# Rotary embeddings of a two-layer hybrid decoder: halves turned by SBUF transfers in place of permutation products

## The chip, the cores and the metric

One core of a Trainium2 chip runs the whole program. The metric is the device time of one execution in microseconds. The kernel before took 964.73 us (median of 3 runs, 963.35 to 967.94). The instructions run on five engines: PE (TensorE, its weight loads shown apart as PEld), DVE (VectorE), ACT (ScalarE), POOL (GpSimd) and SP (SyncE), which here only starts transfers.

## The reference

Two layers over 256 positions of width 1024, in float32. Each layer has a mixer sub-layer with three branches (a linear recurrence, retention, latent attention) that share one input projection, then a gated MLP. Three tensors of the mixer are rotated by position:

```python
def apply_rope(x, cos, sin):
    half = x.shape[-1] // 2
    x1, x2 = x[..., :half], x[..., half:]
    return jnp.concatenate([x1 * cos - x2 * sin, x1 * sin + x2 * cos], axis=-1)

q = apply_rope(q.reshape(b, s, 8, 64), cos, sin)      # retention, halves of 32
k = apply_rope(k.reshape(b, s, 8, 64), cos, sin)
k_rope = apply_rope(kr, cos, sin)                     # latent attention, one key of 32, halves of 16
q_rope = apply_rope(q_rope, cos, sin)                 # eight queries of 32, halves of 16
```

## The kernel before

Activations lie with features on the 128 partitions and the 256 positions along the row. Every dense product is made of three products of float32r parts (a high and a low part of the weights, the same of the activations), so each 1 MB block of weights is loaded into one of three `raw` slots by SP, split into `w_hi` by ACT (line 598) and `w_lo` by DVE (line 1097), and then used by PE (line 1697). A slot is loaded again when the low part of its block is made (`lo_ready`), and its high part is overwritten when PE has used it (`blk_used`). SP's list of loads (line 480) is in the order of the blocks, and each of its waits holds everything behind it. The order of work on every engine is written out by hand. The blocks of a mixer layer are, by number: 0, 1 values; 2, 3 retention queries; 4, 5 retention keys; 6, 7 recurrence inputs (`lx`); 8, 9, 10 latents (`c`), the last one with the rotary key; 11, 12 retention gates (`g`); 13, 14 recurrence gates (`lg`); 15, 16 latent queries up (`uq`); 17 latent keys and values up (`ukv`); 18 on: merge gates and output projections by turns. A block of 256 columns is `two_tiles`, 48 products.

The rotation. For the retention queries and keys there are four pairs of tiles, 0 to 3, which PE leaves in banks 2, 4, 5 and 0. DVE multiplies a pair by the cosines into `AB` and by the sines into one of two halves of `tmp` (`rope_parts`, lines 1305 and 1306). PE multiplies `tmp` with a signed permutation table (`rotate`, line 1809, a float32 product of 512 columns) into the bank it came from, and DVE adds that bank to `AB` (`rope_sum`, line 1311). `rotate(0)` and `rotate(1)` stand ahead of block 6 on PE, `rotate(2)` ahead of block 7, `rotate(3)` ahead of block 8. DVE's order around them is: split 5, parts 1, split 6, split 7, parts 2, sum 0, parts 3, sum 1, (in layer 0 the angles of the second table), split 8, taps 0, sum 2, split 9, sum 3, taps 1, split 10. After the splits of blocks 7 to 20 DVE also makes one sum of the modulation (line 1090).

The rotary key follows block 10 (`rotary_key_parts`, lines 1392 and 1393, ahead of split 13; the product on line 1862 behind block 11; `rotary_key_sum`, line 1398, behind the first two score tiles). The rotary queries follow block 16 (`rotary_q_parts`, lines 1457 and 1458, ahead of split 19; the product on line 1962; `rotary_q_sum`, line 1463, between `variance(0)` and `variance(1)`, both line 1469). ACT spreads each variance over a tile (line 854), and PE transposes it into a bank (`head_scales`, line 1953) with the value products between them; `head_scales(1)` is the last thing PE does before the merge gates.

The tables (identity, `center`, `mean64`, the two permutations, the decays and the mask) come in two transfers; the second, 1472 KB, is issued by ACT in layer 0 after split 3.

Of the kernel before, what the change touches and what calls it, by code (L numbers as in the profile page):

```python
# [21 lines left out]
P = 128  # L22
# [4 lines left out]
ALU = mybir.AluOpType  # L27
# [27 lines left out]
def constants(seq):  # L55
# [4 lines left out]
    center = ident - same_head / 64.0  # L60
    mean64 = same_head / 64.0
    ones = np.ones((P, P))

    def rotation(dim):
        half = dim // 2
        r = np.zeros((P, P))
        for m in range(P):
            if m % dim < half:
                r[m + half, m] = -1.0
            else:  # L70
                r[m - half, m] = 1.0
        return r
# [8 lines left out]
    inv_ret = (ROPE_THETA ** (-np.arange(0, 64, 2) / 64.0))[f % 32][:, None]  # L81
    inv_mla = (ROPE_THETA ** (-np.arange(0, 32, 2) / 32.0))[f % 16][:, None]
# [3 lines left out]
    parts = [ident, ones, inv_ret, inv_mla, eps, q_eps, tiny, center, mean64, rotation(64), rotation(32), *decay, mask]  # L86
# [33 lines left out]
def trunk_kernel(nc, A, consts, out):  # L120
# [90 lines left out]
    with ctx:  # L211
# [49 lines left out]
        kr = sb("kr", [P, T])  # L261
        rot_tmp = pbuf[:].rearrange("p a b -> p (a b)")[:, 0:2 * T].rearrange("p (a b) -> p a b", a=2)
# [20 lines left out]
        center, mean64, rot_r, rot_m = (piece(NFIRST + P * i) for i in range(4))  # L283
        c0 = NFIRST + 4 * P
# [44 lines left out]
        rot_ps, rot_t, rot_c, rope = sig("rot_ps", 4), sig("rot_t", 4), sig("rot_c", 4), sig("rope", 4)  # L329
# [17 lines left out]
        kt_ps, kt_t, kt_c, kt = (sig(n, 1) for n in ("kt_ps", "kt_t", "kt_c", "kt"))  # L347
        qt_ps, qt_t, qt_c, qt = (sig(n, 1) for n in ("qt_ps", "qt_t", "qt_c", "qt"))
# [106 lines left out]
        def _(sp):  # L455
# [4 lines left out]
            for n in range(ADA0):  # L460
# [98 lines left out]
        def _(act):  # L559
# [178 lines left out]
            for l in range(L):  # L738
# [39 lines left out]
                act.wait_ge(rot_ps.s, rot_ps.at(l, 4))  # L778
# [238 lines left out]
        def _(dve):  # L1017
# [277 lines left out]
            for l in range(L):  # L1295
# [12 lines left out]
                def rope_sum(i):  # L1308
                    dve.wait_ge(rot_ps.s, rot_ps.at(l, i + 1))
# [379 lines left out]
        def _(pe):  # L1689
# [84 lines left out]
            for l in range(L):  # L1774
# [28 lines left out]
                def rotate(i):  # L1803
                    if i == 0:
                        pe.wait_ge(tables_in, 16)
                        pe.wait_ge(v_ev.s, v_ev.at(l, 4))
# [414 lines left out]
```

## Time and profile before

| | |
|---|---|
| median, lowest, highest of 3 runs | 964.73, 963.35, 967.94 us |
| span of the profiled execution, first to last instruction | 962.9 us |
| PE busy | 944.9 us (98%) |
| DVE busy | 723.5 us (75%) |
| ACT busy | 521.0 us (54%) |
| PE weight loads busy | 881.8 us (92%) |
| transfers | 206.37 MB, 214 GB/s |

The profiled execution is told by its span; what lies around the span is not in the page, and the span is 1.8 us below the median of the runs. Busy time is of one engine, so the shares do not add up. Lines are those of the kernel, and many matmuls have the line of a helper (1697). A row of the timeline has start and duration in us, the engine, the line, the operation, what is written and read, how many instructions are merged in it and, in brackets, how long the engine was idle before it and what ended that. SPq and ACTq are the instructions with which SP and ACT start transfers. The two layers run through the mixer 463.9 us apart.

### The profile page before, as it was taken

Reading aid. Unit: us, or ns where it says so; the run is one execution under the profiler, and the core shown is the slowest. Engines: PE = TensorE matmul, PEld = TensorE weight load, DVE = VectorE, ACT = ScalarE, POOL = GpSimd, SP = SyncE. Lnnn points to the kernel's source line nnn. Section 1 sums busy time; section 2 is a strip of 40 time slices with the busy share of each in tenths; the row PEclk is TensorE's granted clock in tenths of the full one; section 3 lists DMA queues with packets and bytes.
Section 4 is the critical chain, followed back from the end, with each engine's and each line's share of the span. In section 5 each row is a group of like instructions: output and inputs, shape, how many; then the busy total and the mean of one; then the engine's idle time right before and its main releaser. Section 6 shows DMA issues by size and latency. Waiting matters only on the chain.

```text
span 962.9 us, 17659 instructions
## 1 busy us (share of the span) xinstructions
PE 944.9 (98%) x6956; PEld 881.8 (92%) x6956; DVE 723.5 (75%) x966; ACT 521.0 (54%) x693; POOL 43.5 (5%) x85
## 2 busy tenths in 40 slices
PE   7999999999999999999999999999999999999997
PEld 7889999999998999999979999999999799999996
DVE  4869968867687878887786976887668787676666
ACT  4345856436457655454673475743445675554553
POOL 0000000100000000000000000000000000000000
PEclk7799999999999999999999999999999999999999
DMA  9986668765584676766546775767657555655451
GB/s 354 328 258 213 229 214 259 244 222 198 179 291 121 233 248 249 252 242 202 203 160 180 244 245 182 245 207 256 201 180 251 175 175 175 208 181 178 144 201 47
DMA packets 134427, 206.37 MB, mean 214 GB/s; under 512 B 6496, under 2 KB 104800, under 8 KB 134240
## 3 DMA queue, kind: packets, MB, share of 16 engines
q1 hardware_dynamic: 122704, 162.08, 51.2%
q0 software_dynamic: 11520, 41.95, 11.9%
q10 hardware_dynamic: 144, 1.51, 0.5%
q8 instruction: 43, 0.70, 0.3%
q14 instruction: 16, 0.13, 0.0%
HBM read 204.47 MB, written 1.05 MB: 213 GB/s over the span
## 4 chain that ended last, share of the span: by engine, by line
PE 89%; DVE 4%; DMA 3%; ACT 1%; issue 1%; SPq 1%; DVEq 0%; ACTq 0%
PE banks L1697 79%; DMA h<-in_ada_rows 1%; DVE w_lo L1097 1%; DMA raw<-in_w_in 1%; PE banks L1713 1%; PE banks L1979 1%; PE banks L1982 1%; PE banks L1721 1%; SPq L463 1%; PE banks L1827 1%; PE banks L1809 1%; PE banks L1989 1%; PE banks L1727 1%; PE banks L1846 1%; DVE EF L1599 1%
## 5 line engine op out<-in xcount | busy, mean ns | idle before, releaser
L1697 PE MATMUL banks<-h_lo,w_hi 128*128 128x256 f32 x1504 | 425.9, 283 | 2.0 <-DVE w_lo L1097 1.8
L1697 PE MATMUL banks<-h_hi,w_lo 128*128 128x256 f32 x1504 | 420.7, 280 | 0.0
L1697 PE MATMUL banks<-h_hi,w_hi 128*128 128x256 f32 x1504 | 420.6, 280 | 0.0
L1697 PEld LDWEIGHTS banks<-h_lo,w_hi 128*128 128x128 f32 x1504 | 283.5, 188 | 5.4 <-DVE w_lo L1097 2.2
L1697 PEld LDWEIGHTS banks<-h_hi,w_lo 128*128 128x128 f32 x1504 | 283.5, 188 | 2.3 <-issue 1.4
L1697 PEld LDWEIGHTS banks<-h_hi,w_hi 128*128 128x128 f32 x1504 | 283.4, 188 | 0.0
L1097 DVE TENSOR_TENSOR w_lo<-raw,w_hi 128x2048 fp32r<-128x2048 f32 x96 | 219.3, 2289 | 51.2 <-ACT w_hi L598 50.9
L598 ACT ACTIVATE w_hi<-raw 128x2048 fp32r<-128x2048 f32 x96 | 182.5, 1912 | 109.8 <-PE banks L1697 85.6
L1599 DVE SCALAR_TENSOR_TENSOR EF<-banks,par,EF 128x254 f32<-128x254 f32 (+1 forms) x176 | 76.8, 478 | 57.2 <-ACT EF L949 52.4
L1623 DVE TENSOR_TENSOR w_lo<-raw,w_hi 128x2048 fp32r<-128x2048 f32 x42 | 96.0, 2285 | 21.5 <-ACT w_hi L968 21.5
L968 ACT ACTIVATE w_hi<-raw 128x2048 fp32r<-128x2048 f32 x42 | 80.4, 1913 | 36.7 <-PE banks L1697 36.7
L949 ACT ACTIVATE EF<-banks,par 128x256 f32<-128x256 f32 x88 | 44.8, 560 | 92.3 <-PE banks L1697 92.3
L1090 DVE SCALAR_TENSOR_TENSOR adw<-adw,cbc 128x1024 f32<-128x1024 f32 x66 | 79.6, 1220 | 1.2 <-DVE h L1537 1.1
L1697 PE MATMUL banks<-w_hi,oa_lo 128*128 128x512 f32 x192 | 75.9, 395 | 0.0
L1697 PE MATMUL banks<-w_hi,oa_hi 128*128 128x512 f32 x192 | 75.9, 395 | 0.0
L1697 PE MATMUL banks<-w_lo,oa_hi 128*128 128x512 f32 x192 | 75.9, 395 | 0.0
L542 POOL DMA_DIRECT2D adw<-in_ada_rows x80 | 42.3, 529 | 694.5 <-DVE adw L1090 493.4
L876 ACT ACTIVATE lat<-banks 128x512 f32<-128x512 f32 x24 | 14.2, 592 | 74.8 <-PE banks L1697 74.8
L1697 PEld LDWEIGHTS banks<-w_hi,oa_hi 128*128 128x128 f32 x192 | 36.1, 188 | 8.6
L1697 PEld LDWEIGHTS banks<-w_lo,oa_hi 128*128 128x128 f32 x192 | 36.1, 188 | 7.9
L1697 PEld LDWEIGHTS banks<-w_hi,oa_lo 128*128 128x128 f32 x192 | 36.1, 188 | 7.8
L1697 PE MATMUL banks<-oa_lo,w_hi 128*128 128x256 f32 x128 | 36.9, 288 | 0.0
(277 smaller groups left out, 1242.5 us busy)
## 6 DMA issues: line engine op xcount, KB each, us to landing
raw<-in_w_in SPq DMA_DIRECT2D x52, 1024.0 KB, 5.5
raw<-in_ffn_w_up SPq DMA_DIRECT2D x44, 1024.0 KB, 5.1
adw<-in_ada_rows POOLq DMA_DIRECT2D x80, 512.0 KB, 4.8
raw<-in_ffn_w_down SPq DMA_DIRECT2D x22, 1024.0 KB, 4.8
raw<-in_w_out SPq DMA_DIRECT2D x8, 1024.0 KB, 7.3
raw<-in_ret_wo SPq DMA_DIRECT2D x4, 1024.0 KB, 6.2
raw<-in_lru_wo SPq DMA_DIRECT2D x4, 1024.0 KB, 6.8
raw<-in_mla_wo SPq DMA_DIRECT2D x4, 1024.0 KB, 7.5
```

Source lines behind the costliest of these rows:

```text
L463: sp.dma_start(ada0_buf(n), src).then_inc(ada0_landed(n)[0], 16)
L542: pool.dma_start(adw[:, slot, :], ada_v[:, bass.ds(n + ADA0, 1), :].rearrange("p a d -> p (a d)")).then_inc(adw_in[slot], 16)
L598: A_(dst, src, ACT.Copy).then_inc(hi_ready.s, 1)
L876: A_(flat2(lat, m % 2), PS[:, gate_bank(m), :], ACT.Tanh, scale=0.5).then_inc(mg_th.s, 1)
L949: a = A_(EF[:, 2 * part + b, :], PS[:, 4 + part, T * b:T * b + T], ACT.Identity, scale=par[:, l, bass.ds(i * 2 + col["tap2"] + NFF * (1 - ...
L968: A_(w_hi[:, slot, :], raw[:, slot, :], ACT.Copy).then_inc(hi_ready.s, 1)
L1090: V.scalar_tensor_tensor(adw[:, n % 2, :], adw[:, n % 2, :], 1.0, cbc[:], ALU.mult, ALU.mult, accum_out=mraw[:, n % NT:n % NT + 1]).then_i ...
L1097: V.tensor_tensor(dst, whole, hi, ALU.subtract).then_inc(lo_ready.s, 1)
L1599: v = V.scalar_tensor_tensor(EF[:, 2 * part + b, d:T], PS[:, 4 + part, T * b:T * b + T - d], par[:, l, bass.ds(i * 2 + col[f"tap{tap}"] + ...
L1623: V.tensor_tensor(w_lo[:, slot, :], raw[:, slot, :], w_hi[:, slot, :].bitcast(F32), ALU.subtract).then_inc(lo_ready.s, 1)
L1697: ins = MM(ps, lhs, rhs, start=first and n == 0, stop=last and n == 2)
L1713: ins = MM(PS[:, bank, P * i:P * i + P], x[:, c, P * kk:P * kk + P], diag[:, c, :], start=True, stop=True)
```

## The change

The products with permutation tables go. DVE's product with the sines (whose table now has a minus for one half of each head, from negative frequencies) is moved between partitions by SP: for each group of `half` partitions one transfer from SBUF to SBUF takes the other half of the head. That is 4 transfers of 32 partitions for each of the four pairs (`turn`), 8 of 16 partitions for the rotary key and 8 for the rotary queries. DVE then adds the landed tile instead of a bank. `turn(0)` stands in SP's list behind the load of block 7, `turn(1)` behind 8, `turn(2)` and `turn(3)` behind 10, the key's behind 15, the queries' behind 21, each with a wait for DVE's product. PE no longer waits for the sums before it writes a bank again, only for DVE's two reads of it. Three tables of 128 columns leave the constants (`center`, which nothing read, and the permutations).

```diff
-    parts = [ident, ones, inv_ret, inv_mla, eps, q_eps, tiny, center, mean64, rotation(64), rotation(32), *decay, mask]
+    parts = [ident, ones, inv_ret, inv_mla, eps, q_eps, tiny, mean64, *decay, mask]
...
+            def halves_turned(dst, src, half, landed_sig):
+                for p in range(0, P, half):
+                    q = p ^ half
+                    sp.dma_start(dst[p:p + half], src[q:q + half]).then_inc(landed_sig.s, 16)
+
+            def turn(l, i):
+                two = slice(2 * (i % 2), 2 * (i % 2) + 2)
+                sp.wait_ge(rot_t.s, rot_t.at(l, i + 1))
+                if i >= 2:
+                    sp.wait_ge(rope.s, rope.at(l, i - 1))
+                halves_turned(lat[:, two, :], tmp[:, two, :], 32, turn_in[i % 2])
...
+                    for i in {7: (0,), 8: (1,), 10: (2, 3)}.get(j, ()):
+                        turn(l, i)
+                    if j == 15:
+                        sp.wait_ge(kt_t.s, kt_t.at(l, 1))
+                        halves_turned(lat[:, 1, :], lat[:, 0, :], 16, kt_in)
+                    if j == 21:
+                        sp.wait_ge(qt_t.s, qt_t.at(l, 1))
+                        halves_turned(turned_q, rot_tmp, 16, qt_in)
...
-                act.wait_ge(rot_ps.s, rot_ps.at(l, 4))
+                act.wait_ge(rope.s, rope.at(l, 4))
...
                     if i >= 2:
-                        dve.wait_ge(rot_ps.s, rot_ps.at(l, i - 1))
+                        dve.wait_ge(turn_in[i % 2].s, turn_in[i % 2].at(l, 64))
...
-                    dve.wait_ge(rot_ps.s, rot_ps.at(l, i + 1))
+                    dve.wait_ge(turn_in[i % 2].s, turn_in[i % 2].at(l, 64 * (i // 2) + 64))
                     dve.wait_ge(rot_c.s, rot_c.at(l, i + 1))
-                    V.tensor_tensor(AB[:, 2 * i:2 * i + 2, :], AB[:, 2 * i:2 * i + 2, :], rope_bank(i), ALU.add).then_inc(rope.s, 1)
+                    V.tensor_tensor(AB[:, 2 * i:2 * i + 2, :], AB[:, 2 * i:2 * i + 2, :], lat[:, 2 * (i % 2):2 * (i % 2) + 2, :],
+                                    ALU.add).then_inc(rope.s, 1)
...
-                    dve.wait_ge(kt_ps.s, kt_ps.at(l, 1))
+                    dve.wait_ge(kt_in.s, kt_in.at(l, 128))
...
-                    dve.wait_ge(qt_ps.s, qt_ps.at(l, 1))
+                    dve.wait_ge(qt_in.s, qt_in.at(l, 128))
...
-                    MM(PS[:, (2, 4, 5, 0)[i], :], rot_r, flat2(tmp, i % 2), start=True, stop=True).then_inc(rot_ps.s, 1)
-                rotate(0)
-                rotate(1)
+                pe.wait_ge(v_ev.s, v_ev.at(l, 4))
                 two_tiles(l, J[("lx", 0)], 3)
-                rotate(2)
                 two_tiles(l, J[("lx", 1)], 1)
-                rotate(3)
-                pe.wait_ge(rope.s, rope.at(l, 2))
+                heads_taken(1)
                 two_tiles(l, J[("c", 0)], 4)
...
-                MM(PS[:, 2, 0:T], rot_m, lat[:, 0, :], start=True, stop=True).then_inc(kt_ps.s, 1)
...
-                MM(PS[:, 4, :], rot_m, rot_tmp.rearrange("p a b -> p (a b)"), start=True, stop=True).then_inc(qt_ps.s, 1)
```

`heads_taken(i)` waits for the two products of pair `i` on DVE. The turned queries land in `ptb`, the turned pairs in `lat` rows 0 to 3, the turned key in `lat` row 1.

## Rows read from the trace of the kernel before

**Rows 1.** The page, part 1: busy us, share of the span, instructions.

```profile
PE 944.9 (98%) x6956; PEld 881.8 (92%) x6956; DVE 723.5 (75%) x966; ACT 521.0 (54%) x693; POOL 43.5 (5%) x85
```

**Rows 2.** Windows: stretch, length; busy per engine; granted clock, DMA share, GB/s.

```profile
0.00:44.00 44.00, 36.59 (x157) 33.13 (x158) 29.28 (x58) 20.21 (x34) 1.57 (x6) 0.73 0.92 337
...
72.00:96.00 24.00, 24.00 (x193) 22.71 (x192) 23.38 (x50) 13.34 (x18) 1.58 (x3) 1.00 0.65 217
```

**Rows 3.** Chain of work, layer 1: start us, us on the chain, what.

```profile
534.86 1.72 PE banks L1809 x4
...
542.18 0.86 PE banks L1809 x2
...
549.55 11.21 PE banks L1697 x96
...
575.42 0.43 PE banks L1862 x2
...
613.22 0.86 PE banks L1962 x2
...
618.22 0.44 PE banks L1953 x4
```

**Rows 4.** The same chain in layer 0.

```profile
70.97 1.72 PE banks L1809 x4
...
85.61 11.21 PE banks L1697 x96
...
98.54 5.61 PE banks L1697 x48
```

**Rows 5.** Timeline of DVE, layer 0.

```profile
63.45 0.68 DVE L1306 TENSOR_TENSOR tmp<-banks,sinr 128x512 f32<-128x512 f32 x1
...
72.92 0.68 DVE L1305 TENSOR_TENSOR AB<-banks,cosr 128x512 f32<-128x512 f32 x1
...
80.94 2.28 DVE L1097 TENSOR_TENSOR w_lo<-raw,w_hi 128x2048 fp32r<-128x2048 f32 x1
...
95.89 1.22 DVE L1106 TENSOR_TENSOR w_lo<-raw,w_hi 128x1024 fp32r<-128x1024 f32 x1
...
106.86 0.42 DVE L1393 TENSOR_TENSOR lat<-banks,sinm 128x256 f32<-128x256 f32 x1
...
113.86 0.41 DVE L1398 TENSOR_TENSOR kr<-kr,banks 128x256 f32<-128x256 f32 x1
```

**Rows 6.** Timeline of DVE, layer 1, the split of block 9.

```profile
547.41 2.28 DVE L1097 TENSOR_TENSOR w_lo<-raw,w_hi 128x2048 fp32r<-128x2048 f32 x1
```

**Rows 7.** Timeline of DVE, layer 1, around the rotary queries.

```profile
611.22 0.68 DVE L1458 TENSOR_TENSOR pbuf<-banks,sinm 128x512 f32<-128x512 f32 x1
...
615.29 0.63 DVE L1463 TENSOR_TENSOR AB<-AB,banks 128x512 f32<-128x512 f32 x1
615.84 0.19 DVE L1469 RECIPROCAL var_rc<-var_sd 128x8 f32<-128x8 f32 x1
```

**Rows 8.** Timeline of ACT in the same stretch.

```profile
615.41 1.30 ACT L854 ACTIVATE lat<-var_rc 128x512 f32<-128x512 f32 x2 [0.23 <-DVE var_rc L1469]
```

**Rows 9.** Timeline of SP: transfers started one behind the other.

```profile
1.33 0.42 SPq L457 DMA_DIRECT2D cst<-shape_constants  x1
1.79 0.43 SPq L459 DMA_DIRECT2D x<-in_x  x1
...
512.00 1.28 SPq L491 DMA_DIRECT2D wbd<-in_lru_wx  x2
```

**Rows 10.** Transfers: KB each, median us from issue to landing.

```profile
out<-x SPq DMA_DIRECT2D x4, 256.0 KB, 2.0
...
wbd<-in_lru_wx SPq DMA_DIRECT2D x4, 64.0 KB, 5.6
```

**Rows 11.** Timeline of ACT, layer 0, the split of block 4.

```profile
53.56 1.92 ACT L598 ACTIVATE w_hi<-raw 128x2048 fp32r<-128x2048 f32 x1 [10.64 <-DMA raw<-in_w_in]
```

**Rows 12.** Timeline of PE, layer 0, block 4.

```profile
57.86 0.38 PE L1697 MATMUL banks<-h_lo,w_hi 128*128 128x256 f32 x1 [1.76 <-DVE w_lo L1097]
```

More of the change, by code:

```diff
@@ L59, in constants @@
     same_head = (f[:, None] // 64 == f[None, :] // 64).astype(np.float64)
-    center = ident - same_head / 64.0
     mean64 = same_head / 64.0
     ones = np.ones((P, P))
[L64 to L72, printed above, removed]
     t = np.arange(seq)[None, :]
@@ L80, in constants @@
     mask = np.concatenate([diag, np.zeros((P, P)), diag], axis=1)
-    inv_ret = (ROPE_THETA ** (-np.arange(0, 64, 2) / 64.0))[f % 32][:, None]
-    inv_mla = (ROPE_THETA ** (-np.arange(0, 32, 2) / 32.0))[f % 16][:, None]
+    inv_ret = ((ROPE_THETA ** (-np.arange(0, 64, 2) / 64.0))[f % 32] * np.where(f % 64 < 32, 1.0, -1.0))[:, None]
+    inv_mla = ((ROPE_THETA ** (-np.arange(0, 32, 2) / 32.0))[f % 16] * np.where(f % 32 < 16, 1.0, -1.0))[:, None]
     eps = np.full((P, 1), EPS)
@@ L282, in trunk_kernel @@
         inv_ret, inv_mla, eps, q_eps, tiny = (piece(2 * P + i, 1) for i in range(5))
-        center, mean64, rot_r, rot_m = (piece(NFIRST + P * i) for i in range(4))
-        c0 = NFIRST + 4 * P
+        mean64 = piece(NFIRST)
+        c0 = NFIRST + P
         decay = cst[:, c0:c0 + HEADS * T].rearrange("p (h t) -> p h t", h=HEADS)
@@ L328, in trunk_kernel @@
         g_th, g_ev = sig("g_th", 2), sig("g_ev", 2)
-        rot_ps, rot_t, rot_c, rope = sig("rot_ps", 4), sig("rot_t", 4), sig("rot_c", 4), sig("rope", 4)
+        rot_t, rot_c, rope = sig("rot_t", 4), sig("rot_c", 4), sig("rope", 4)
+        turn_in = [sig(f"turn_in{i}", 128) for i in range(2)]
         rs_ps, rs_p, rs_av = sig("rs_ps", 8), sig("rs_p", 8), sig("rs_av", 8)
@@ L346, in trunk_kernel @@
         uv_ps, uv_ev = sig("uv_ps", 1), sig("uv_ev", 2)
-        kt_ps, kt_t, kt_c, kt = (sig(n, 1) for n in ("kt_ps", "kt_t", "kt_c", "kt"))
-        qt_ps, qt_t, qt_c, qt = (sig(n, 1) for n in ("qt_ps", "qt_t", "qt_c", "qt"))
+        kt_in, kt_t, kt_c, kt = sig("kt_in", 128), *(sig(n, 1) for n in ("kt_t", "kt_c", "kt"))
+        qt_in, qt_t, qt_c, qt = sig("qt_in", 128), *(sig(n, 1) for n in ("qt_t", "qt_c", "qt"))
         s_ps, s_m, s_max, s_neg = (sig(n, 4) for n in ("s_ps", "s_m", "s_max", "s_neg"))
@@ L1874, in _ @@
                 ins.then_inc(cs_ps.s, 1)
-                pe.wait_ge(kt.s, kt.at(l, 1))
+                pe.wait_ge(kt_t.s, kt_t.at(l, 1))
+                pe.wait_ge(kt_c.s, kt_c.at(l, 1))
                 two_tiles(l, J[("g", 1)], 2)
@@ L1938, in head_means @@
                 def head_means(i):
+                    if l == 0 and i == 0:
+                        pe.wait_ge(tables_in, 16)
                     pe.wait_ge(rv_sq.s, rv_sq.at(l, i + 1))
@@ L2028, in merge_gate @@
                         ready(l, gj)
-                        sg, n = ((qt, 1), (r_o, 1), (uv_ev, 2), (mg_th, 2))[m] if m < 4 else (mg_th, m - 1)
+                        sg, n = ((qt_t, 1), (r_o, 1), (uv_ev, 2), (mg_th, 2))[m] if m < 4 else (mg_th, m - 1)
                         pe.wait_ge(sg.s, sg.at(l, n))
+                        if m == 0:
+                            pe.wait_ge(qt_c.s, qt_c.at(l, 1))
                     wh, wl = weights(l, gj)
```

20 lines of the change are left out of this document (9 added, 11 removed).

## The prediction

> **What bounds the kernel now.** I read the page's busy times first: PE is busy for 98% of the span, DVE for 75% [rows 1]. The windows then say whether the stretches with the rotations are like the whole. From 72 to 96 us PE is busy for all of 24.00 us at the full granted clock, but DVE for 23.38 of 24, far over its mean [rows 2]. So in layer 0 the cover for DVE's work is thin just where the change takes PE's work away. The chain of waits gives what a product is worth: it runs through PE in both layers, and a piece's length on it is what PE would gain without the piece [rows 3, 4]. The timelines of DVE, ACT, PE and SP then say who is late next.
>
> **What the change removes.** On the chain two rotations take 1.72 us and a single one 0.86 [rows 3]; there are four per layer, 3.44 us. The key's product takes 0.43, the queries' 0.86 [rows 3]. That is 4.73 us per layer and 9.46 in both, if everything else were early enough. It is not, so I follow the places where PE must meet somebody.
>
> **Layer 1, up to the queries.** Without rotations block 8 could start at 549.55 - 3.44 = 546.11 [rows 3] and block 9 half a pair of blocks (11.21 / 2 = 5.60) later, at 551.7. DVE makes the low part of block 9 by 547.41 + 2.28 = 549.69 [rows 6], and it is DVE's own full list that sets this time, not PE. PE arrives 2 us later than that, so nothing is lost: 3.44 us gained. Behind block 11 the waits of DVE and ACT are for PE's products, so they move with it, and the key's 0.43 comes on top: 3.87 us.
>
> **Layer 0, up to the queries.** Here DVE has the angles of the second table to make between sum 1 and split 8. PE ends the keys at 70.97 [rows 4]. Blocks 6 and 7 run directly, 2 x 5.60, to 82.2. The low part of block 8 is ready at 80.94 + 2.28 = 83.22 [rows 5], so PE starts it at about 83.3 and ends block 9 at 94.5 or a little later. The two gate products before block 10 take 1.73 (98.54 less the end of the pair of blocks, 85.61 + 11.21 = 96.82 [rows 4]), to 96.2, and block 10 is ready at 95.89 + 1.22 = 97.11 [rows 5]. DVE's full list sets that one too. It starts at 97.15 where it started at 98.54 [rows 4]: 1.39 us of the 3.44 are kept, and 2.05 lost to DVE. With the key's 0.43 that is 1.82. All this goes with DVE's list unmoved, which needs the turned halves to be there in time.
>
> **Do the turns land in time?** The trace has no transfer from SBUF to SBUF, so I bound them. An issue on SP: two ordinary ones stand 0.46 us apart (1.33 and 1.79), two of the 64 KB blocks with a more broken pattern take 1.28, 0.64 each [rows 9]. I take 0.5. From issue to landing: 2.0 us for a plain store of 256 KB on a quiet queue, 5.6 for 64 KB right behind a 1 MB load [rows 10]. `turn(1)` is issued once DVE's sine product of pair 1 is done, at 63.45 + 0.68 = 64.13 in layer 0 [rows 5], behind load 8; `turn(0)` is a pair earlier. With 4 x 0.64 and the 5.6 us turn 1 is there at 72.3. Its first reader, parts 3, stands behind parts 2 and sum 0, at 72.92 + 3 x 0.6 = 74.7 [rows 5]. Turns 2 and 3 have two splits and more between product and sum. I take zero; if turn 1 needs the 10.64 us that ACT once waited for a load [rows 11], it lands at 77.3, 2.6 us late, and that is the other end. The load behind the turns: 256 KB more on the queue is 0.26 / 0.337 = 0.8 us at the rate of the first window [rows 2]. That is block 8's in both layers; SP issues it more than two splits of DVE's list ahead of its own, so I take zero, with 0.8 as the end. The key's eight: issued from 106.86 + 0.42 = 107.28, the last at 107.3 + 3.5 = 110.8, landed at 112.8. Its sum starts at 113.86 before [rows 5] and can now move up by less than 1 us. So zero too, up to 0.5. DVE's sums have two SBUF inputs instead of SBUF and a bank; operations of this size that read a bank take 0.63 to 0.68 [rows 7], and I change nothing for it.
>
> **The rotary queries are the place where it costs.** I work in layer 1's old time, since all engines arrive shifted alike. DVE's product is done at 611.22 + 0.68 = 611.90 [rows 7]. SP has by then issued load 21 and stands at the wait. The eighth transfer is issued at 611.9 + 7 x 0.5 = 615.4 and lands 2.0 later, at T = 617.5 with a little for the semaphore. The sum was due at 615.29 [rows 7]. DVE stands for 2.2 us, and behind it stands `variance(1)`, 0.55 after the sum's start, 0.19 long [rows 7]; ACT then needs 0.65 for its tile (1.30 for two [rows 8]), with about 0.16 for the two handovers. So `head_scales(1)` on PE starts at T + 1.55 = 619.05, where it started at 618.22 [rows 3]. The 0.86 us of the product are gone and 0.83 on top. The bounds: with 0.64 per issue and 5.6 to landing T is 622.0 and the loss 5.3. On the good side a transfer that never touches HBM could be quicker than any row, and the end is the product's whole 0.86 gained; less is likely even then, since ACT's two tiles, ready at 615.41 + 1.30 = 616.7 [rows 8], are themselves set by DVE. What is late next behind it is the low part of block 20, which follows the second `group_norm`: two operations of DVE of 0.7 and a split of 2.28 [rows 5], 3.7 us, while PE has the first merge gate to do, a block of 5.6. Load 22, pushed back by up to 2 us, is for the merge product after the next.
>
> The trace shows that SP's transfers are issued without waiting for one another's landing [rows 9]. The Trainium skill, page "DMA: Bandwidth & Descriptors", section "Rules for kernel authors", says that many small transfers should be coalesced, since "under 64 KB you're paying mostly overhead", and these are of 16 and 32 KB; section "Anatomy of one DMA" puts the fixed part at about 2.0 us. If the eight paid that one after the other, the sum would be the third rival's, by an estimate from that page 16.6 us for the eight; if they overlap as the rows' issues do, it stays as above.
>
> **The constants.** 3 x 64 KB less in the second table, on the same engines as the loads of blocks 4 and 5. ACT waits 10.64 us for block 4 in layer 0 [rows 11], and PE 1.76 behind it [rows 12]. 0.196 MB at 337 GB/s [rows 2] is 0.58 us; I take 0.5, between 0 and 0.6. It moves PE and DVE alike, so it adds to the above.
>
> **The sum.** Layer 0: 0.5 + 1.82 - 0.83 = 1.5. Layer 1: 3.87 - 0.83 = 3.0. Together 4.5 us off the profiled span of 962.9, 958.4; the median of the runs lies 1.8 above the span, so 964.7 - 4.5 = 960.2. Best of the bounds: 6.2 + 2 x 0.86 + 0.1 = 8.0 off, 956.7. Worst: 0 for the constants, 5.7 - 2 x 5.3 - 0.5 - 2.6 - 0.8 = 8.8 slower, 973.5.
>
> **Rivals.**
> 1. PE's whole 9.46 us come back, 955.3. It needs DVE's list in layer 0 to be looser than it looks, and the queries to land before 615.3. For it speaks only the 98% [rows 1]; against it the ends of the splits [rows 5] and the 3.4 us between product and sum [rows 7], less than eight issues. 0.10.
> 2. The queries land late because of the 1 MB load just ahead of them in the same queue, about 4 us after the last issue, midway between the two rows: T about 619.6, loss 2.9 per layer, together 6.2 - 5.8 = 0.4, so 964.3, no change. For it: 5.6 us of the small transfers behind a load [rows 10]. Against it: SP issues load 21 while DVE is still before its two products, so that load should be nearly through when the eighth is issued. 0.20.
> 3. Slower: each of the eight takes the fixed 2.0 us [rows 10] in turn and not side by side. T is 627.9, `head_scales(1)` 629.5, 11.2 us lost per layer: 6.2 - 22.4 = 16.2 slower, 981. It becomes a loss from the point where T passes 619.8 (618.22 + 3.1 - 1.55), that is from 0.81 us per issue on with 2 us for the last landing. This is the page's rule as a mechanism here. Milder forms of it (around 1.3 us each, 972) are in its chance, 0.10.
> 4. DVE stands at parts 3 in layer 0 for turn 1, by the 2.6 us worked out above, all of it on PE: 962.8. For it: DVE's list has no gap there [rows 2]. Against it: 2.4 us between the slower landing and the reader. 0.12.
>
> **How the numbers follow.** The forecast has 0.48, with a range of its own from 958 to 962.5. A difference under 0.5% (4.8 us) is about what a measurement of this kernel can't tell from none: that is 959.9 to 969.6. The forecast lies at the edge of it; I put a bit under three fifths of its 0.48 below 959.9 together with rival 1 and a share of the uncertainty of the baseline: faster 0.41. Slower holds the larger part of rival 3: 0.09. The rest, with rivals 2 and 4, is no change: 0.50. The range from 956.5 to 966.0 leaves out rival 3, most of rival 1 and a little of rival 2.
>
> **What would show it.** Right: no PE time on lines 1809, 1862 and 1962; PE waiting in layer 0 for `w_lo` ahead of blocks 8 to 10, some 2 us in all, and not in layer 1; DVE waiting for a transfer at line 1463's sum in both layers, by 2 us or so, and PE waiting before the second set of line 1953; no wait of DVE at the parts and sums of the four pairs. Wrong: a wait of DVE for transfers ahead of the split of block 8; issues on SP over 0.81 us each; PE not waiting at line 1953 at all (then 958 or less); or PE's saved time given back in the MLP, where I assume that everybody follows PE.

## The result and the profile after

The change makes the kernel slower. The changed kernel takes 974.71 us (median of 4 runs, 973.80 to 975.97), the kernel before 964.77 us in the same comparison; the ratio is 1.0101, with a 95% interval of 1.0083 to 1.0119. The forecast was 960.2 us and its range ended at 966.0. The profiled execution has a span of 972.4 us; before it was 962.9. One of the ten executions of e1 below took 1304.61 us at a mean granted clock of 0.65; it moves e1's median by under 0.1 us.

The page's first part, as in [rows 1], and three of its transfer rows (KB each, median us from issue to landing, as in [rows 10]):

```profile
PE 940.3 (97%) x6932; PEld 880.3 (91%) x6932; DVE 723.3 (74%) x966; ACT 520.9 (54%) x693; POOL 43.5 (4%) x85
...
lat<-tmp SPq DMA_DIRECT2D x32, 64.0 KB, 5.6
...
ptb<-pbuf SPq DMA_DIRECT2D x16, 32.0 KB, 4.0
lat<-lat SPq DMA_DIRECT2D x16, 16.0 KB, 3.4
```

PE is busy for 4.6 us less, though 9.46 us of products are gone. A busy time that falls by half of what was taken away says that some of the rest got slower. The span grew by 9.5 us all the same, so PE stands for 14 us more than before.

To see where, I set PE's timelines side by side and took the start of the same product in both. The table has the times of the profiled executions; a minus means that the changed kernel is ahead.

| what PE starts | layer 0, before, after | shift | layer 1, before, after | shift |
|---|---|---|---|---|
| recurrence gates, ahead of block 10 | 96.65, 93.80 | -2.85 | 560.60, 562.79 | +2.19 |
| first score tile | 111.84, 108.88 | -2.96 | 575.78, 577.54 | +1.76 |
| third score tile, 1.3 us behind the scale broadcast | 121.98, 120.14 | -1.84 | 585.93, 589.24 | +3.31 |
| `head_scales(1)` | 154.11, 157.44 | +3.33 | 618.06, 626.02 | +7.96 |
| attention scores, behind block 18 | 168.72, 174.33 | +5.61 | 632.67, 642.25 | +9.58 |
| end of the layer | | +5.70 | | +9.5 |

From the end of one mixer to the start of the next nothing moves. Each layer gains 3 to 4 us up to the scores, and loses at three places: between the first and the third score tile (1.1 and 1.55 us), at `head_scales(1)` (5.17 and 4.65 us net of the removed product), and right behind it (2.28 and 1.62 us).

**The gap at `head_scales(1)`.** DVE, SP and PE in layer 1; the rows answer to [rows 7] and to the last of [rows 3]:

```profile
614.57 0.68 DVE L1475 TENSOR_TENSOR pbuf<-banks,sinm 128x512 f32<-128x512 f32 x1
615.17 2.29 DVE L1110 TENSOR_TENSOR w_lo<-raw,w_hi 128x2048 fp32r<-128x2048 f32 x1
617.38 1.22 DVE L1103 SCALAR_TENSOR_TENSOR adw<-adw,cbc 128x1024 f32<-128x1024 f32 x1
...
618.53 0.20 DVE L1485 RECIPROCAL var_rc<-var_sd 128x8 f32<-128x8 f32 x1
624.50 0.69 DVE L1480 TENSOR_TENSOR AB<-AB,ptb 128x512 f32<-128x512 f32 x1 [5.78 <-DMA ptb<-pbuf]
625.11 0.20 DVE L1485 RECIPROCAL var_rc<-var_sd 128x8 f32<-128x8 f32 x1
```
```profile
613.00 0.37 SPq L485 DMA_DIRECT2D raw<-in_w_in  x1
615.28 5.31 SPq L464 DMA_DIRECT2D ptb<-pbuf  x8
620.71 0.51 SPq L485 DMA_DIRECT2D raw<-in_ret_wo  x1
```
```profile
619.44 0.66 PE L1963 MATMUL banks<-cst,lat 128*128 128x128 f32 x4 [0.57 <-ACT lat L867]
...
626.02 0.67 PE L1963 MATMUL banks<-cst,lat 128*128 128x128 f32 x4 [4.53 <-ACT lat L867]
```

The product ends at 615.25, SP issues eight transfers in 5.3 us (6.7 in layer 0), and the sum starts at 624.50, 9.25 us behind the product (9.8 in layer 0). DVE stands for 5.78 us with nothing that it could do, because its list is fixed: the second variance, 0.2 us long, stands behind the sum. PE is released by ACT, which is released by that variance. The row at 619.44 shows a second, smaller wait: without the queries' product PE also stands 0.57 us ahead of `head_scales(0)`, in both layers. A reader who sees "[4.53 <-ACT lat L867]" must follow it two steps to find the transfer. The waits (who, for whom: total us, times, longest) show the same chain:

```profile
ACT lat L867 <- DVE var_rc L1485: 14.3, 4, 6.5
...
DVE AB L1480 <- DMA ptb<-pbuf: 12.1, 2, 6.3
...
PE banks L1963 <- ACT lat L867: 10.7, 4, 5.1
```

**The slow clock.** Windows of the changed kernel, with columns as in [rows 2]. First layer 0 behind the gap, then layer 1 in the stretch of the one-column sums and block 12, then layer 1 around its gap:

```profile
154.00:156.00 2.00, 0.00 (x0) 0.00 (x0) 0.08 (x1) 0.00 (x0) 0.00 (x0) 0.87 0.90 237
156.00:158.00 2.00, 0.56 (x3) 0.56 (x4) 1.97 (x4) 1.24 (x2) 0.00 (x0) 0.50 0.78 302
158.00:160.00 2.00, 2.00 (x11) 2.00 (x10) 1.38 (x4) 2.00 (x3) 0.00 (x0) 0.50 0.00 0
160.00:162.00 2.00, 2.00 (x12) 2.00 (x11) 2.00 (x2) 1.98 (x4) 0.00 (x0) 0.50 0.00 0
```
```profile
580.00:582.00 2.00, 2.00 (x19) 2.00 (x19) 1.09 (x2) 2.00 (x2) 0.00 (x0) 1.00 0.91 359
582.00:584.00 2.00, 2.00 (x12) 2.00 (x11) 1.79 (x1) 1.88 (x4) 0.00 (x0) 0.54 0.01 2
584.00:586.00 2.00, 2.00 (x13) 2.00 (x12) 2.00 (x5) 0.00 (x0) 0.00 (x0) 0.61 0.32 33
...
622.00:624.00 2.00, 0.00 (x0) 0.00 (x0) 0.00 (x0) 0.00 (x0) 0.00 (x0) 1.00 0.88 301
...
626.00:628.00 2.00, 1.98 (x12) 1.98 (x13) 1.82 (x3) 2.00 (x2) 0.00 (x0) 0.63 0.18 70
628.00:630.00 2.00, 2.00 (x11) 2.00 (x11) 2.00 (x2) 1.98 (x5) 0.00 (x0) 0.51 0.01 3
630.00:632.00 2.00, 2.00 (x19) 2.00 (x19) 2.00 (x4) 1.08 (x1) 0.00 (x0) 1.00 0.30 27
```

The third number from the end of each row is the granted clock as a share of the full 2.4 GHz. At 0.50 (the level of 1.2 GHz) PE is "busy" for the whole of 2.00 us but starts 11 or 12 products, where it starts 19 at 1.00. In the kernel before, the same stretches of work stand at 1.00.

### The profile page after: what moved, and what is told of

Its sections match the earlier page's. It is cut to its first block, busy times and chain, and to the rows that moved or that the text cites. A ratio compares the mean times of both kernels' runs of the same rounds, so it can differ in the third digit from the quotient of the medians.

```text
span 972.4 us, 17675 instructions
## 1 busy us (share of the span) xinstructions
PE 940.3 (97%) x6932; PEld 880.3 (91%) x6932; DVE 723.3 (74%) x966; ACT 520.9 (54%) x693; POOL 43.5 (4%) x85
## 4 chain that ended last, share of the span: by engine, by line
PE 80%; DVE 8%; DMA 5%; issue 3%; SPq 2%; ACT 2%; DVEq 0%; ACTq 0%
PE banks L1713 72%; DVE w_lo L1110 2%; DMA raw<-in_w_in 2%; SPq L464 1%; DMA h<-in_ada_rows 1%; DVE adw L1103 1%; ACT w_hi L611 1%; PE banks L1729 1%; PE banks L1986 1%; PE banks L1989 1%; DMA ptb<-pbuf 1%; PE banks L1737 1%; SPq L454 1%; PE banks L1996 1%; PE banks L1743 1%
```

## The experiments

All times below are medians beside runs of the kernel before on the same chip (964.9 to 965.3 us); the ratio is to those runs, with its 95% interval. "Gap" is the time from the end of DVE's sine product of the queries to the start of its sum. Of the eighteen runs e16 and e18 repeat e11 and e14, and e15 the kernel before.

**Which rotation costs (e1, e2).** The queries, and then the queries and the key, are turned by a product with a swap table again; the signed sines stay.

```diff
-                    if j == 21:
-                        sp.wait_ge(qt_t.s, qt_t.at(l, 1))
-                        halves_turned(turned_q, rot_tmp, 16, qt_in)
...
+                MM(PS[:, 4, :], rot_m, rot_tmp.rearrange("p a b -> p (a b)"), start=True, stop=True).then_inc(qt_ps.s, 1)
```

> The changed kernel, but the rotary queries alone are turned by PE's product again (one 64 KB table comes back). Theory (the 9.5 us are lost where DVE stands for the turned queries ahead of the second variance, and in the slower PE clock behind that gap): PE no longer waits at the second head_scales, the 5.3 and 4.8 us there and the 2.3 and 1.6 us behind it go, the 0.86 us product comes back twice. Total 960 to 962 us against 964.8 before. Rival (the small transfers cost by loading the queue of the weights, wherever they stand): three quarters of the moved bytes are still there, so most of the loss stays, 970 us or more.

> The changed kernel with the rotary queries and the rotary key turned by PE's products; only the four pairs of retention tiles are turned by transfers. Theory: the 1.1 us wait (layer 0) and the 1.55 us of slow clock (layer 1) behind the key go too, its 0.43 us product comes back twice: 958 to 960 us, 1 to 2 us under the run with the queries' product alone. Rival (the key's stretch is a matter of the clock's phase and not of its transfers): the same as that run, 960 to 962. Rival (queue load): no better than 968.

e1: 962.64 us, 0.9967 (0.9951 to 0.9983). e2: 960.77 us, 0.9958 (0.9935 to 0.9981). So the queries' transfers, as they are read here, cost 12 us, and without them the change is a gain of 0.3 to 0.4%. The key's turn by product or by transfers makes no difference that is clear of noise: the intervals of e1 and e2 overlap. In e2's profile layer 1 gains 3.3 us (-0.81 at the end of layer 0, -4.11 at the end), which is the 3.44 us of the four pairs' products but for 0.1. In e1 the stretch from the one-column sums to the scale broadcast takes 9.48 and 11.05 us where it took 7.94: the slow clock, without any gap of PE.

**The same transfers, read later (e3, e4).** The only edit of e3 is the place of one line on DVE; e4 moves the key's sum too, behind the recurrence's last operation.

```diff
                 variance(0)
-                rotary_q_sum()
                 variance(1)
...
                 ret_low(0)
                 ret_low(1)
+                rotary_q_sum()
```

> The changed kernel with one line moved: DVE's sum of the queries stands behind the two ret_low operations instead of ahead of the second variance. All transfers stay. Theory: the landing 9 us after the product is hidden, since its reader is 12 us later; 959 to 961 us. Rival (queue load): nothing gained, 974. Rival (the second variance is late for another reason, ACT's chain): PE still waits more than 2 us at the second head_scales, 968 or more.

> As the run with the late query sum, and DVE's sum of the key moved behind the recurrence's l_v, ahead of the third score. Theory: the wait for the key's landing goes too; 957 to 959 us, under the run with the late query sum alone by 1 to 2 us. Rival (the key's stretch costs by the clock's phase alone): no difference from that run within 0.7 us.

e3: 962.43 us, 0.9961 (0.9948 to 0.9975). e4: 961.85 us, 0.9965 (0.9949 to 0.9981). DVE in e3, layer 1:

```profile
614.77 0.69 DVE L1490 TENSOR_TENSOR tmp<-CD,banks 128x512 f32<-128x512 f32 x1 [1.34 <-PE banks L1963]
...
621.53 1.29 DVE L1497 TENSOR_TENSOR oa_lo<-tmp,oa_hi 128x512 fp32r<-128x512 f32 x2
622.74 0.68 DVE L1480 TENSOR_TENSOR AB<-AB,ptb 128x512 f32<-128x512 f32 x1
```

No wait in front of the sum, 12.85 us behind the product: the transfers land 3.2 to 4.9 us after their issue, about as before (3.6 to 5.1), and nobody notices. e3 gives 12.3 us back, more than the change had lost, so the loss was the place of one reader and not the work of the transfers. e4 shows no further gain clear of noise.

**What makes the landing late (e5, e6, e7).** e5 issues load 21 behind the eight transfers in place of ahead of them. e6 makes four transfers of 32 partitions out of the eight, and e7 one transfer of the whole tile; both move the same bytes, but without the exchange of neighbouring groups of 16.

```diff
-            sp.dma_start(block_shape(raw, l, j), src(l)).then_inc(slot_in(l, j), 16)
             if j == 21:
                 sp.wait_ge(qt_t.s, qt_t.at(l, 1))
                 halves_turned(turned_q, rot_tmp, 16, qt_in)
+            sp.dma_start(block_shape(raw, l, j), src(l)).then_inc(slot_in(l, j), 16)
```
```diff
-                        halves_turned(turned_q, rot_tmp, 16, qt_in)
+                        halves_turned(turned_q, rot_tmp, 32, qt_in)            # e6
+                        sp.dma_start(turned_q, rot_tmp).then_inc(qt_in.s, 16)  # e7
```

> The changed kernel with the load of block 21 issued behind the eight transfers of the queries instead of ahead of them. Measured: the time from the end of DVE's sine product to the start of the sum (9.2 us in the changed kernel, of which 5.1 for the issues). If the transfers stand in the queue behind the 1 MB load, it falls to about 7 us and the total by 4 us, to 970. If their landing takes 4 us by itself (completion, or one port for 16 partitions), it stays at 9 and the total at 974.

> The changed kernel, the queries moved by four transfers of 32 partitions instead of eight of 16 (the halves of 32 partitions change places instead of those of 16, so the queries' rotation is not the reference's; same bytes). If the issues are in series at 0.63 us and the landing follows the last one, the time from product to sum falls by 2.5 us, to 6.7, and the total by 5 us, to 970. If the landing is set by the load ahead in the queue or by bytes, it stays near 9.

> The changed kernel, the queries copied by one transfer of 128 partitions, unturned (so their rotation is not the reference's; same bytes). If count sets it: 0.6 for the issue and 4 to land, 4.7 us from product to sum, total about 966. If the load ahead in the queue sets it: the load of block 21 is issued 2.4 us before the product ends and lands 5 to 7 us after its issue, so 3 to 5 us from product to sum here too, and only the run with the load behind the turn tells. If bytes or the port set it: 9.

| | median us | ratio | gap, layer 0, 1 | landing, layer 1: min/median/max |
|---|---|---|---|---|
| changed kernel | 974.71 | 1.0101 | 9.8, 9.25 | 3.6/4.1/5.1 |
| e5 | 972.13 | 1.0076 (1.0053 to 1.0098) | 8.9, 8.57 | 1.9/2.5/4.1 |
| e6 | 972.03 | 1.0059 (1.0033 to 1.0084) | 9.06, 8.80 | 3.6/5.2/5.7 |
| e7 | 969.09 | 1.0042 (1.0024 to 1.0059) | 7.58, 6.45 | one: 6.4 |

Neither the load ahead nor the number alone explains the gap. With half the transfers it shrinks by 0.45 and 0.7 us only; one of the four issues in layer 1 took 1.81 us, and the landing grew. With a single transfer it shrinks by 2.8 us in layer 1 and 2.2 in layer 0, the most of the three, and still that transfer takes 6.4 us to land (7.5 in layer 0). In e5 the first ones land after 1.9 us and the last after 4.1: something else was in their way.

**Loads held back (e12, e17).** In e12 SP waits for the eight to land before it issues load 21. In e17 DVE's modulation sum of block 19 is moved behind the queries' sum as well; POOL issues its next 512 KB load when that is done, so this load starts later too.

```diff
                         halves_turned(turned_q, rot_tmp, 16, qt_in)
+                        sp.wait_ge(qt_in.s, qt_in.at(l, 128))
...
-                mixer_split(l, 19)
+                split_block(l, 19)
                 variance(0)
                 rotary_q_sum()
                 variance(1)
+                if 19 in mixer_sums:
+                    ada_sum(l, mixer_sums[19])
```

> The changed kernel, with load 21 and those behind it held back in the queue until the eight transfers of the queries have landed. Theory: 0.6 us per issue is fixed, but the last landing (4.1 us after its issue) is long because a 1 MB load moves on the same engines; with the queue empty it takes 2.0 to 2.5 us and the gap on DVE from the product's end to the sum is 7.0 to 7.3 us where it was 9.25 and 9.8; 970 us, if load 22 still comes in time. Rival: the landing is slow by itself (a transfer of small rows between partitions), the gap stays at 8.6 us as in e5 and the held loads come late as well: 973 us or more.

> As e12, and the adw reduction of block 19 is moved behind the queries' sum, so that the 512 KB load on POOL's queue that it sets off is issued after the transfers have landed too. Theory: with no load in flight the last transfer lands about 2 us after its issue, like the first ones (1.9 us); the gap from the product's end to the sum is 6.7 to 7.0 us where e12 had 8.55 and 8.7. Rival: 4 us is the price of the last of eight small transfers whatever moves beside it; the gap stays at 8.5 us. In either case the moved reduction puts 1.2 us behind the sum, so the whole time stays near e12's, 971 to 973 us.

e12: 973.36 us, 1.0083 (1.0069 to 1.0098). e17: 965.85 us, 1.0011 (0.9996 to 1.0026). SP, POOL and DVE in layer 1, and the landings (us, min/median/max), in e12:

```profile
614.62 4.94 SPq L464 DMA_DIRECT2D ptb<-pbuf  x8
```
```profile
618.63 0.53 POOL L556 DMA_DIRECT2D adw<-in_ada_rows  x1 [4.04 <-DVE adw L1104]
```
```profile
623.01 0.69 DVE L1481 TENSOR_TENSOR AB<-AB,ptb 128x512 f32<-128x512 f32 x1 [4.99 <-DMA ptb<-pbuf]
```
```profile
DMA to landing us min/median/max: 1.9/2.4/4.0
```

The same in e17:

```profile
612.14 4.95 SPq L464 DMA_DIRECT2D ptb<-pbuf  x8
```
```profile
621.10 0.53 POOL L556 DMA_DIRECT2D adw<-in_ada_rows  x1 [8.98 <-DVE adw L1104]
```
```profile
618.46 0.69 DVE L1481 TENSOR_TENSOR AB<-AB,ptb 128x512 f32<-128x512 f32 x1 [4.07 <-DMA ptb<-pbuf]
```

The gap is 8.47 us in e12 (614.54 to 623.01) and 6.40 in e17 (612.06 to 618.46); in layer 0 it is 8.64 and 6.45. The eight issues take 4.95 us in both in layer 1. What differs is the end: the last transfer starts at 619.0 in e12, 0.4 us behind POOL's load, and the sum follows 4.0 us later; in e17, where POOL's last load was issued at 611.6, it starts at 616.5 and the sum follows 2.0 us later. So the theory of e17 holds, and the forecast's "2.0 later" is right where no load is issued close by. My expectation of the time was wrong: I wrote 971 to 973. The modulation sum that I counted as 1.2 us of loss stands beside ACT's and PE's work behind the variance, the gap is 2.1 to 2.2 us shorter per layer, PE's 0.57 us ahead of `head_scales(0)` are gone too, since the first variance no longer stands behind the modulation sum, and the clock does not fall behind the gap in layer 1 (+1.92 at `head_scales(1)`, +1.98 at the attention scores, where e12 has +6.47 and +8.07). In layer 0 it does fall behind a gap of 2.5 us on PE, and 1.7 us are lost.

**The clock behind the gap (e8).** Ten dummy products of 256 columns are put where PE would stand.

```diff
                     if c == 1:
+                        pe.wait_ge(qt_t.s, qt_t.at(l, 1))
+                        pe.wait_ge(qt_c.s, qt_c.at(l, 1))
+                        keep_going(4, 10)
                     head_scales(c)
```

> The changed kernel with ten products of the identity table with the first tables (128 by 256 columns, into a free bank, read by nobody; 0.43 us each on PE) ahead of the second head_scales, where PE stands idle for 4.5 us. Theory: the granted clock falls because PE stood idle, so with the gap filled it stays at 2.4 GHz and the 2.3 and 1.6 us behind the gap go, while the gap itself stays: 970 to 972 us. Rival: the clock falls there anyway, or the dummy products delay PE: 975 or more.

971.82 us, 1.0061 (1.0044 to 1.0078). In layer 1 the distance from `head_scales(1)` to the attention scores grows by 0.06 us in place of 1.62, and the clock stays:

```profile
626.00:628.00 2.00, 2.00 (x11) 1.77 (x10) 0.00 (x0) 0.00 (x0) 0.00 (x0) 1.00 0.89 309
...
630.00:632.00 2.00, 1.46 (x12) 1.09 (x11) 1.83 (x5) 1.77 (x2) 0.00 (x0) 1.00 0.39 147
```

In layer 0, where the gap is longer, 1.6 us are still lost. There the eight land up to 6.8 us after their issue, the sum comes 12.3 us behind the product, and PE still stands for 3.3 us. The profiled execution was the slowest of nine (977.86 us), with 4.6 us of falls in the key's stretches. So the cost behind the gap goes with PE's standing still, 1.4 to 2.6 us in the eight gaps of 3.7 to 5.1 us that the changed kernel, e5, e6 and e12 have. That products which compute nothing save part of it rests on the median of nine executions, 2.9 us below the changed kernel's, with intervals apart. One profiled gap alone would not show it: behind gaps of 1.7 us (e7, layer 1) and 2.5 us (e17, layer 1) the clock stayed up as well, and behind e17's other gap of 2.5 us it fell.

**The clock where PE does not stand (e9 to e11, e13 to e16, e18).** In the changed kernel's layer 1, and in e1 and e3, the clock falls in block 12, behind the one-column sums (ten products, twenty rows of the trace), though PE has no gap. The key's product stood just ahead of them before. e9 (on e3) and e10 (on e4) put a dummy product of 256 columns in its place; e11 is e3 with the key turned by the product, without its transfers. e13 is e3 with the key's transfers in use and its product made as well, unread. e14, and e18 again, are e3 with neither; they leave the key's rotation out. e15 is the kernel before and e16 is e11, once more.

```diff
                 two_tiles(l, J[("g", 0)], 4)
+                pe.wait_ge(kt_t.s, kt_t.at(l, 1))
+                pe.wait_ge(kt_c.s, kt_c.at(l, 1))
+                keep_going(2, 1)                                          # e9, e10
+                MM(PS[:, 2, 0:T], rot_m, lat[:, 0, :], start=True, stop=True)   # e11, e13
                 pe.wait_ge(rope.s, rope.at(l, 4))
...
-                    V.tensor_tensor(kr[:], kr[:], lat[:, 1, :], ALU.add).then_inc(kt.s, 1)
+                    V.tensor_tensor(kr[:], kr[:], PS[:, 2, 0:T], ALU.add).then_inc(kt.s, 1)  # e11
+                    V.tensor_tensor(kr[:], kr[:], lat[:, 0, :], ALU.add).then_inc(kt.s, 1)   # e14, e18
```

> One product of 256 columns, whose result nobody reads, is put where the key's product with the permutation stood; for the rest it is the kernel with the late query sum (e3). Theory: the fall of the clock in the stretch of the one-column sums comes from PE's thinner work there once the key's product is gone, so the filler brings back what the product did for the clock: sums to scale broadcast 7.95 us in both layers where e3 had 9.49 and 9.54, granted clock 1.00, at a price of 0.43 us per layer; about 2.2 us faster than e3, 960 us, 0.994 of the kernel before. Rival: the fall has another cause (the place of the DVE sums, chance from run to run); then the clock falls in at least one of the two stretches and the filler is 0.9 us of loss, 963 us.

> The kernel with both sums late (e4) and the same filler product. Theory: no fall of the clock in either key stretch, as in e4's own profile, so the filler costs its 0.43 us per layer in the profiled run, and in the median it gives back what e4 loses when its clock falls: 960 to 961 us. Rival: the filler is pure loss in the median too, 962.7 us.

> The key is rotated by the product as before, the four pairs by transfers, the queries by transfers with their sum moved behind the low parts of the retention output. Theory: keeps all that the transfers give where they are hidden (4.1 us of pairs and 1.7 us of the queries' product over both layers) and neither the wait nor a fall of the clock: 5 us faster than before, 959.5 us, ratio 0.9945, the fastest of all. Rival: the late sum costs what the queries' product cost, as DVE is no freer there: 960.8 us, the same as with both products on PE.

> The key is turned by the eight transfers, which the sum reads, and the product with the permutation is made too, on its real operands and in its old place, read by nobody; the queries' sum is late as in e3. If it is the product's absence that lets the clock fall in the stretch of the one-column sums (and the dummy product failed because its operands were others), the stretch takes 7.94 us in both layers. If it is the key's transfers, or chance, it takes about 9.5 us in at least one of the two.

> As e3, but the key is turned neither by a product nor by transfers: its sum adds the unturned product, so the key's rotation is left out. If the key's transfers bring the fall of the clock, the stretch takes 7.94 us in both layers; if the product's absence does, about 9.5 us in both or in one of two; if chance, either.

> The kernel before once more, for the clock in the stretch of the one-column sums: 7.94 us in both layers if the product or the absence of transfers protects it; if the falls are chance, one or the other layer shows about 9.5 us with some one in two.

> The kernel with the key by product and the late query sum once more: 7.94 us in both layers if the product or the absence of the key's transfers protects the clock there; otherwise about 9.5 us in some of them.

> The kernel of e14 once more (the key's rotation is left out). If the product's absence alone lets the clock fall, the stretch takes about 9.5 us in both layers again; if it is chance, 7.94 us in one of them or both.

e9 962.10 us, 0.9967 (0.9955 to 0.9978); e10 961.58, 0.9961 (0.9948 to 0.9973); e11 960.85, 0.9959 (0.9945 to 0.9972). The others have one time each (e13 960.76, e14 962.48, e15 963.51, e16 960.87, e18 963.78 us) and are read for the clock alone. The filler's theory fell: e9 takes 9.49 and 9.50 us in the stretch. The tally over all profiles, two layers each:

| key turned by | kernels | stretches in which the clock fell |
|---|---|---|
| product alone | before, e2, e11, e15, e16 | 0 of 10 |
| transfers alone | changed, e1, e3 to e8, e12, e17 | 10 of 20 |
| transfers, with a product that nobody reads | e9, e10, e13 | 4 of 6 |
| neither | e14, e18 | 4 of 4 |

A fall lengthens the stretch by 1.5 us, or by 3.1. The same stretch of layer 1 in e14 and in e16:

```profile
574.00:576.00 2.00, 2.00 (x15) 2.00 (x16) 0.97 (x2) 2.00 (x3) 0.00 (x0) 0.75 0.43 170
576.00:578.00 2.00, 2.00 (x11) 2.00 (x11) 1.49 (x1) 1.97 (x4) 0.00 (x0) 0.50 0.00 0
578.00:580.00 2.00, 2.00 (x18) 2.00 (x17) 2.00 (x5) 0.21 (x2) 0.00 (x0) 0.90 0.23 18
```
```profile
574.00:576.00 2.00, 2.00 (x19) 2.00 (x19) 1.01 (x2) 2.00 (x2) 0.00 (x0) 1.00 0.34 135
576.00:578.00 2.00, 2.00 (x19) 2.00 (x18) 1.87 (x1) 1.79 (x4) 0.00 (x0) 1.00 0.00 0
578.00:580.00 2.00, 2.00 (x20) 2.00 (x19) 2.00 (x5) 0.00 (x0) 0.00 (x0) 1.00 0.19 31
```

PE is busy for all of both, so no view of waits or idle time shows this loss: only the granted clock and the number of products in a window do. The transfers are not needed for it (e14 and e18 have none), and an unread product does not prevent it.

The tally looks as if the key's product protected the clock, but it can't show that. In each profile the moments at which the granted clock changes are whole multiples of one step apart, and where this beat lies against the kernel's work differs from profile to profile. I took the first moment of the beat behind the start of the one-column sums in each of the 40 stretches. In 22 of them it comes 0.38 to 1.81 us behind, and the clock fell in none: the ten with the product alone, ten with transfers alone (the changed kernel's layer 0 among them, 1.39) and two with the unread product. In the other 18 it lies outside that range, and the clock fell in all of them. Every stretch with the product alone happens to be among the 22, so the moment tells the falls apart without an exception and the way the key is turned does not. This is the rival that the expectations of e2 and e4 call the clock's phase, and it fits best. Whether the product does anything at all stays open, and so does another difference: with the product alone PE waits for DVE's sum of the key and not only for its two reads. The times speak against a large effect: e3 is at 0.9961 without the product and e11 at 0.9959 with it.

In e1, e3, e9, e10, e14 and e18 the clock also fell in layer 0 behind PE's wait of 1.9 to 2.2 us for the low part of block 8, and from there to the recurrence gates PE takes 12.8 to 12.9 us where it takes 11.9 to 12.0 without the fall.

**The best version.** e2, e4, e10 and e11 lie between 960.8 and 961.9 us with overlapping intervals; I can't rank them. Each beats the kernel before by about 0.4% and the changed one by 13 to 14 us. Turning the queries by transfers with a late reader (e11) is worth next to nothing over their product (e2): from layer 0's attention scores to layer 1's, e11 gains 3.43 us and e2 3.29. PE's wait of 0.57 us ahead of `head_scales(0)`, which e11 has and e2 has not, takes the rest of the product's 0.86 back.

## Why the prediction was wrong

The forecast was 4.5 us off the span; it came out 9.5 us longer, 14.0 us apart. From the table of PE's starts, as the prediction's own steps:

| step (a minus is a gain, us) | forecast | measured, layer 0 and 1 | part of the miss |
|---|---|---|---|
| constants, pairs and key's product | -2.32, -3.87 | -2.96, -3.94 | -0.7 |
| key stretch | 0, 0 | +1.12, +1.55 | +2.7 |
| queries, net at `head_scales(1)` | +0.83, +0.83 | +5.17, +4.65 | +8.2 |
| behind `head_scales(1)` | 0, 0 | +2.28, +1.62 | +3.9 |
| the rest of each layer | 0, 0 | +0.09, -0.1 | 0.0 |

**The step that failed** is the one under "The rotary queries are the place where it costs": "The eighth transfer is issued at 611.9 + 7 x 0.5 = 615.4 and lands 2.0 later, at T = 617.5". The place, the chain from the sum over the variance and ACT's tile to PE, and the formula were right. With the measured 9.25 us from product to sum, T is 621.15 in the old time and the formula gives a loss of 621.15 + 1.55 - 618.22 = 4.5 us; 4.65 was measured. The mis-sized term is T: 3.65 us too early. The last issue starts 4.7 us behind the first where I had 3.5, 0.67 us each and not 0.5 (6.0 in layer 0, where one issue took 1.56); it was issued at 620.0 and the sum came 4.5 us later where I had 2.0. I took the issue spacing of plain loads and the landing on a quiet queue [rows 9, 10], the good end twice, although 0.64 for a broken pattern and 5.6 behind a load stood in the same rows. With those the prediction had worked out T = 622.0 and a loss of 5.3 per layer, and put too little on it. In layer 0 the same formula gives 5.0 from the gap of 9.8 us, and 5.17 was measured.

**The clock was missing from the sum.** I priced a late PE at its idle time. The changed kernel loses another 2.28 and 1.62 us behind its two gaps, and 1.1 and 1.55 us in the key's stretch. In the latter, layer 0's part is a plain gap at the full clock. The key's sum starts 8.4 us behind its product, where I had the halves landed 5.5 behind it and a loss of "up to 0.5"; DVE waits, and the scale broadcast comes late:

```profile
114.18 0.42 DVE L1415 TENSOR_TENSOR kr<-kr,lat 128x256 f32<-128x256 f32 x1 [2.66 <-DMA lat<-lat]
```
```profile
118.69 0.71 PE L1887 MATMUL banks<-cst,lat_rc 128*128 128x128 f32 x4 [0.81 <-DVE lat_rc L1429]
```

In layer 1 it is the clock, by the moment at which the stretch came and not by a wait. The worst case of the prediction, 973.5 or 8.8 us slower, was worked out without the clock and was passed: 974.71 was measured, and the span is 9.5 us longer.

**What was right.** Layer 1 gained 3.51 us up to the gates where 3.44 were forecast. The pairs' turns made no engine wait in either layer (rival 4 fell), so the halves that have two splits between product and sum do come in time. DVE's full list held PE up in layer 0 and not in layer 1, for 1.72 us ahead of block 8 and 0.36 ahead of block 9, together 2.08 where 2.05 were forecast:

```profile
81.89 0.36 PE L1713 MATMUL banks<-h_lo,w_hi 128*128 128x256 f32 x1 [1.72 <-DVE w_lo L1110]
```

The key's product came back whole in layer 1 (3.94 less 3.51 is its 0.43). No time was given back in the MLP. In layer 0 the clock's falls in the first 62 us differ between profiles, and the gates start anywhere from 93.8 to 95.9 us in the kernels with turned pairs (profiles without a fall at block 8), and at 96.65 and 95.05 in the two profiles of the kernel before, so the 0.5 us for the constants can't be told apart.

**What the sum took for granted.** The queries' 0.86 us count as a gain in full. They are worth only 0.14 us where the landing is hidden (e11 against e2), because PE then waits ahead of `head_scales(0)` for the first variance. The formula's 4.5 against the measured 4.65 does not see this, since `head_scales(1)` hangs on the late sum alone.

**The rivals.** Rival 2 had the right mechanism, the landing delayed by loads, but 1.6 us too little of it (T at 619.6 against 621.15): the load that matters most is not SP's load 21, worth 0.7 to 0.9 us (e5), but POOL's 512 KB load, worth 2.1 to 2.2 (e12 against e17). Rival 3, every transfer paying in turn, is wrong as a mechanism: in e17 the eight are started in 4.4 us and the last lands 2.0 us after its start, while eight fixed costs of 2.0 in a row would be 16. Its milder form at 972 was near the time for another reason, and that is luck. Its turning point of 0.81 us per issue is 0.84 by its own numbers ((619.77 - 2.0 - 611.9) / 7), which changes nothing here. The Trainium skill, page "DMA: Bandwidth & Descriptors", section "Rules for kernel authors", says that small transfers mostly pay overhead, so that fewer and larger ones should be used; the trace agrees in part. Each one costs SP 0.6 us. Four in place of eight bought 0.45 to 0.7 us of the gap, one in place of eight 2.2 to 2.8 us of it and 5.6 us of the kernel's time, but that one still landed after 6.4 us or more beside the loads. The 2.0 us in the prediction's estimate of 16.6 us stand in the Trainium skill, page "DMA: Bandwidth & Descriptors", section "Anatomy of one DMA", for transfers that GpSimd issues; SP issued these.

## What to carry to other kernels

Before a product is replaced by a round trip through the transfers, count from the last instruction that makes the data to the first that reads it: for the queries it took 6.4 us with the next two loads held back, 9.3 to 9.8 beside them and 12.3 once (e8, layer 0). A reader needs that much other work ahead of it; e3's stands 12.85 us behind the product and never waited. Moving it, one line, was worth 12.3 us. A queue is not the only thing that delays a small transfer: look for every load, from every engine, that is in flight when it is issued. Price a gap on PE at its idle time and the slow clock behind it, and look at the granted clock even where PE is busy throughout. Before a variant is credited with keeping the clock up, look at when the clock could have changed in its profiles: five profiles of the kind that seemed safe had all met the harmless moment.

## What the runs showed of the hardware

- Behind the eight PE gaps of 3.7 to 5.1 us of the changed kernel, e5, e6 and e12 the clock was granted at half for some 3 to 7 us, and 1.4 to 2.6 us were lost. It also fell behind gaps of 2.9 us (e7, layer 0), 2.5 us (e17, layer 0) and 1.9 to 2.2 us (block 8 of six profiles), but not behind 2.5 us (e17, layer 1) and 1.7 us (e7, layer 1).
- It also fell with PE busy throughout, behind four score products and ten products of one column, in 18 of 40 stretches. The moment of the stretch against the beat of the clock's changes tells the 18 from the 22 without an exception; the variant does not.
- An issue of an SBUF to SBUF transfer of 16 partitions by SP mostly took 0.51 to 0.59 us, starts 0.63 apart; single ones took 0.96 to 1.56 (changed kernel), and one of 32 partitions 1.81 (e6). A plain load of 1 MB mostly took 0.37. Landing took 1.9 us at best and 4.0 beside a 512 KB load issued 0.4 us earlier.
